# RWKV stage of a hybrid decoder step: the projection matmuls that are woven between its products, as 24 blocks of twelve per head pair instead of 48 blocks of six

## The reference, cut to what matters

```python
def step(S, inp):
    r_t, w_t, k_t, v_t, av_t, bv_t = inp
    sa = jnp.einsum('bhvk,bhk->bhv', S, av_t)
    S = S * w_t[:, :, None, :] + sa[..., None] * bv_t[:, :, None, :] + v_t[..., None] * k_t[:, :, None, :]
    return S, jnp.einsum('bhvk,bhk->bhv', S, r_t)
...
br = jnp.einsum('btnw,nwd->btnd', branches, p['w_branch'])
gates = jax.nn.sigmoid(gt.reshape(B, T, N_BRANCH, D_MODEL))
mix = jnp.sum(gates * br, axis=2) @ p['w_out']
```

## Time and profile before

| | |
|---|---|
| median of the three runs | 2814.52 us |
| span of the profiled execution | 2809.2 us |
| TensorE busy | 2484.5 us, 88% of the span |
| VectorE busy | 1546.0 us, 55% |
| ScalarE busy | 859.9 us, 31% |
| mean granted TensorE clock | 0.944 |
| start of s0t in pairs 1 and 6 (counted from 0) | 819.30 us, 1273.54 us |

### The profile page before, as it was taken

How to read it: one execution, slowest core, us unless ns; L and a number is a source line. 1 busy time by engine, 2 the same in 40 slices (tenths; PEclk the granted TensorE clock), 3 DMA queues, 4 the chain that set the end, 5 groups by cost and what they waited for, 6 DMA issues and landing times.

```text
span 2809.2 us, 50485 instructions
## 1 busy us (share of the span) xinstructions
PE 2484.5 (88%) x19707; PEld 2325.8 (83%) x19707; DVE 1546.0 (55%) x2210; ACT 859.9 (31%) x940; POOL 98.5 (4%) x171
## 2 busy tenths in 40 slices
PE   5999999456788998889989989599999999999976
PEld 4799999334677887777879989499999999999975
DVE  4533344513565566656663443766666666666665
ACT  4333333222222122222232333233333333333323
POOL 2000000010000000000000000000000000000001
PEclk9999999669899999999999999699999999999987
DMA  5544444244121223223235444144444444444441
GB/s 184 182 145 149 141 149 149 64 158 149 43 85 58 89 86 119 68 69 101 72 98 164 149 131 150 34 147 145 143 151 148 149 149 149 146 151 145 142 133 49
DMA packets 280233, 346.61 MB, mean 123 GB/s; under 512 B 6735, under 2 KB 240511, under 8 KB 278381
## 3 DMA queue, kind: packets, MB, share of 16 engines
q1 hardware_dynamic: 270365, 308.44, 34.5%
q0 software_dynamic: 9712, 36.30, 4.0%
q10 hardware_dynamic: 32, 0.01, 0.0%
HBM read 333.83 MB, written 10.89 MB: 123 GB/s over the span
## 4 chain that ended last, share of the span: by engine, by line
PE 71%; DVE 14%; issue 6%; ACT 5%; DMA 3%; DVEq 1%; POOL 1%; ACTq 0%; SPq 0%; POOLq 0%
PE bank L225 21%; PE bank L227 20%; PE bank L226 20%; PE bank L1015 5%; ACT hi L209 2%; DVE lo L216 2%; DMA work<-in_cache_mem_k 2%; DVE rw L1799 1%; DVE work L775 1%; PE bank L1384 1%; DVE q L701 1%; PE bank L424 1%; DVE rw L1797 1%; ACT rw L1741 1%; DMA raw<-in_w_in 0%
## 5 line engine op out<-in xcount | busy, mean ns | idle before, releaser
L225 PE MATMUL bank<-ah,hi 128*128 128x320 f32 x3232 | 1027.9, 318 | 45.2 <-DVE lo L216 21.1
L216 DVE TENSOR_TENSOR lo<-raw,hi 128x2048 fp32r<-128x2048 f32 x286 | 655.6, 2292 | 667.6 <-ACT hi L209 653.3
L226 PE MATMUL bank<-al,hi 128*128 128x320 f32 x3232 | 1006.5, 311 | 0.0
L227 PE MATMUL bank<-ah,lo 128*128 128x320 f32 x3232 | 1006.2, 311 | 0.0
L209 ACT ACTIVATE hi<-raw 128x2048 fp32r<-128x2048 f32 x286 | 547.6, 1915 | 1300.2 <-PE bank L227 1267.9
L225 PEld LDWEIGHTS bank<-ah,hi 128*128 128x128 f32 x3232 | 613.8, 190 | 65.9 <-issue 49.8
L226 PEld LDWEIGHTS bank<-al,hi 128*128 128x128 f32 x3232 | 614.5, 190 | 1.4 <-issue 0.2
L227 PEld LDWEIGHTS bank<-ah,lo 128*128 128x128 f32 x3232 | 614.0, 190 | 0.0
L225 PE MATMUL bank<-bh,hi 128*128 128x320 f32 x1088 | 346.9, 319 | 19.3 <-DVE bl L1814 18.5
L226 PE MATMUL bank<-bl,hi 128*128 128x320 f32 x1088 | 337.2, 310 | 0.0
L227 PE MATMUL bank<-bh,lo 128*128 128x320 f32 x1088 | 337.2, 310 | 0.0
(11 more groups left out here) (335 smaller groups left out, 1791.3 us busy)
## 6 DMA issues: line engine op xcount, KB each, us to landing
raw<-in_w_in SPq DMA_DIRECT2D x98, 1024.0 KB, 5.3
raw<-in_w_up SPq DMA_DIRECT2D x88, 1024.0 KB, 5.1
raw<-in_w_down SPq DMA_DIRECT2D x44, 1024.0 KB, 5.1
raw<-in_w_branch SPq DMA_DIRECT2D x24, 1024.0 KB, 5.5
raw<-in_w_out SPq DMA_DIRECT2D x16, 1024.0 KB, 5.4
raw<-in_w_mem_k SPq DMA_DIRECT2D x8, 1024.0 KB, 5.5
raw<-in_w_mem_v SPq DMA_DIRECT2D x8, 1024.0 KB, 5.1
work<-in_cache_mem_k POOLq DMA_DIRECT2D x8, 1024.0 KB, 5.3
```

The lines of the kernel that those rows point to most:

```text
L216: dve.tensor_tensor(lo[c % NS][:, :], raw[c % 2][:, :], hi[c % NS][:, :], ALU.subtract)\
L225: pe.matmul(out, a_hi, b_hi, start=first, stop=False)
L226: pe.matmul(out, a_hi, b_lo, start=False, stop=False)
L227: return pe.matmul(out, a_lo, b_hi, start=False, stop=last)
```

## The change

`pe_group_steps` hands back control after every fourth k instead of every second, so a block has twelve matmuls (4 k by 3 passes) instead of six, and there are 24 blocks per pair instead of 48. The table `STEPS` is written anew for them. No matmul, copy, transfer or buffer is added or taken away.

```diff
-                        if k % 2:
+                        if k % 4 == 3:
                             yield
...
-        STEPS = {PR["s0t"]: 1, PR["bonus"]: 2, PR["A"]: 1, PR["B"]: 7, PR["Bk"]: 1, PR["Cb"]: 1, PR["beT"]: 1,
-                 PR["kaT"]: 1, PR["R1"]: 1, PR["RT1"]: 1, PR["A4"]: 1, PR["B4"]: 3, PR["Q"]: 1, PR["Q2"]: 1,
-                 PR["QT2"]: 2, PR["QT4"]: 3, PR["W1"]: 2, PR["W2"]: 1, PR["S0"]: 1, PR["X1"]: 1, PR["X2"]: 1,
-                 PR["SA2"]: 2, PR["SA3"]: 1, PR["S3"]: 1, PR["S4"]: 2, PR["mean"]: 2, PR["tr1"]: 2, PR["var"]: 2,
-                 PR["g"]: 2}
-        assert sum(STEPS.values()) == 48
-        UNIT_END = [next(p for p in range(NPR) if sum(STEPS.get(x, 0) for x in range(p + 1)) >= 8 * (j + 1)) for j in range(6)]
+        STEPS = {PR["s0t"]: 1, PR["bonus"]: 1, PR["A"]: 1, PR["B"]: 2, PR["Cb"]: 1, PR["beT"]: 1, PR["A2"]: 1, PR["R1"]: 1,
+                 PR["A4"]: 1, PR["R2"]: 1, PR["Q"]: 1, PR["Q2"]: 1, PR["QT4"]: 1, PR["W1"]: 1, PR["W2"]: 1, PR["S0"]: 1,
+                 PR["X1"]: 1, PR["SA2"]: 1, PR["S3"]: 1, PR["S4"]: 1, PR["mean"]: 1, PR["tr1"]: 1, PR["g"]: 1}
+        assert sum(STEPS.values()) == 24
+        UNIT_END = [next(p for p in range(NPR) if sum(STEPS.get(x, 0) for x in range(p + 1)) >= 4 * (j + 1)) for j in range(6)]
```

## The result

The changed kernel takes 2884.33 us (median of 4 runs, 2876.15 to 2886.96), the kernel before 2812.87 us beside it. The ratio is 1.0242, with a 95% interval of 1.0226 to 1.0258: slower by 68 us by the ratio, by 71.5 us between the medians.

What follows compares the result with a forecast made beforehand. TensorE was taken to set the pace, through its matmuls, changes between matmul kinds and waits for VectorE. Waits and places (+34 us) and the clock (+21 us) added 55 to 2814.5, giving 2870 us, range 2845 to 2890.

Steps and rivals of the forecast that it cites:

- Units served elsewhere (part 2): In each pair, units' hi and lo served at other products: 11.9 us of new waits, 5.9 us gone.
- five of six places of service: Opening claim on the pair: the change moves five of six places where serving a unit costs TensorE its full length.
- The wait ahead of the next pair's first block: Ahead of s0t at the turn of a pair: the wait of 1.35 us for lo goes.
- the 1.4 for X2, SA3 and Bk: These copies lose the block ahead of them while VectorE has other work: 1.4 us of new wait per pair together.
- Fewer places (part 1): Six fewer places per pair where a block stands beside a product: 1.8 us given back, bounds nothing and 1.9.
- The 0.32 us per place: At Bk: a product beside a block costs 0.93 us, one without 0.61, so a place is worth 0.32.
- The sum of parts 1 and 2: Waits and places together: 11.9 - 5.9 - 1.8 = +4.2 us per pair, +34 us for eight pairs.
- The clock (part 3): After the wait at Q2: one more fall to 1.2 GHz in every pair, 2.6 us each, 21 us in all.
- the first rival: No further fall of the clock, perhaps as falls beside SA1 go with its wait: 2849 us, chance 0.22.
- The rival without a further fall: The same as the first rival: no further fall of the clock, only part 2 left, 2849 us, chance 0.22.
- The rival with two further falls: Waits at X0 and SA4, beside thin products, bring a second fall in each pair: 2890 us, chance 0.15.
- The faster rival: Service doesn't hold copies up at Q2, X0, RT1 and SA4 (9.3 us per pair): 2774 us, chance 0.03.

Runs made afterwards that it cites:

- two_places: tuned_a with its two groups of six blocks at s0t and A given in halves to s0t, bonus, A and B; 2724.31 us against 2725.29.
- fill_q2: The changed kernel with 27 more matmuls of 128x128 by 320, whose result nobody reads, ahead of TensorE's wait at Q2; 2861.03 us, ratio 1.0170.
- serve_u2: The changed kernel with only unit 2 served at QT2 instead of Q; 2841.16 us, ratio 1.0100.
- tuned_a: Against the kernel before: blocks of six placed by TensorE's waits, units served at QT, QT4, SA3, SA4, S4 and g; 2725.29 us, ratio 0.9675.

## Why the prediction was right, and where its sizes were off

The forecast of 2870 us had the direction and the mechanism; 2884 us was measured. The number is nearer than its terms were: two terms of the pair's sum were off in opposite directions, and a third fell short.

- **Units served elsewhere (part 2).** The opening says that the change moves five of six places of service; it moves four (units 1 to 4), and the sum rightly works with four. Forecast and measured waits in us: Q2 4.2 and 4.28, X0 2.3 and 2.19, SA4 2.1 and 2.00, SA1 0.4 and 0.43, RT1 1.1 and 0.91. The working from durations of the kernel before held within 0.2 us each. Smaller terms didn't. The wait ahead of the next pair's first block was to go; it shows 0.5 to 2.0 us in most pairs, ended by "issue", which the `lo` of the kernel before had covered. B waits nothing to 1.1 us instead of 1.2, and of the 1.4 for X2, SA3 and Bk only SA3's 0.97 came. Added up over pairs 1 to 6, TensorE's waits over 0.3 us are 9.0 us per pair before and 13.7 after: 4.7 more, where the terms gave 6.0 (11.9 less 5.9).
- **Fewer places (part 1)** gave back less than the 1.8 us per pair that were forecast. A pair is 8.4 us longer. Waits are 4.7 of it and the clock 3.9 (11.4 us more at the lower level, at 0.34), which leaves 0.2 us given back, an estimate with errors of several tenths. Six places at the 0.14 of two_places would give 0.8. The 0.32 us per place was read at one place and is too high for places beside s0t and A; between 64x64 products it was not tried by itself.
- **The sum of parts 1 and 2.** By the price, the 106 us more at the lower level cost 36 us. That leaves 71.7 - 36 = 36 us for waits and places; 34 were forecast. This agreement is partly luck, since the waits were put 1.3 us per pair too high and the places at least 1.0 us too high, and the two nearly cancel.
- **The clock (part 3) was mis-sized.** This is the term that made the forecast 14 us too low. It put one further fall of 6.8 us in each pair, 21 us in all; 36 us came. Six pairs at 0.92 have about 16 us at the lower level each (2 x 0.08 x 99.3) against 5 to 6 before, in two to four falls: after Q2, around X0, and between SA1 and S4. The kernel before has one fall in each of these pairs, beside SA0 or SA1. It went along with SA1's wait, as the first rival had considered, but the one at X0 took its place. The price per microsecond was nearly right (2.55 us for 6.5, 0.39, against 0.34), the number of falls wasn't. The rival with two further falls (2890 us) describes the run better, and it was given 0.15. The rival without a further fall (2849 us) is excluded by the clock after Q2 and by fill_q2. That waits of 2.0 to 2.2 us beside thin products would bring falls was named there and not taken.
- **The faster rival** (service doesn't hold copies up) is excluded by the waits themselves and by serve_u2.

## What to carry to other kernels

Where one table spreads filler work over a dependent chain and another engine's housekeeping hangs on the same table, moving the filler moves the housekeeping. Read which copy stands behind it before joining or moving blocks. In the changed kernel the `lo` that holds up Q2 is done at 1171.6 and first used at 1190.4, ahead of S0. A unit whose buffers aren't needed so soon should be served behind a copy that has cover, not as soon as it can be; in tuned_a two list entries are worth 68 us. A wait of TensorE can cost more than its length: those of 2.0 to 4.3 us here were followed by matmuls at the lower clock in most pairs, at 0.34 us for each microsecond.

## What was not expected of the hardware

The clock fell at short waits too: at X0's wait of 2.19 us in all eight pairs, and at SA4's of 2.00 us in four of seven. Small products stand around both. At the turn of pair 1 the changed kernel waits as long between blocks of 128x128 matmuls, and the clock stays at 1.00:

```profile
930.97 0.41 PE L225 MATMUL bank<-ah,hi 128*128 128x320 f32 x1 [1.98 <-issue]
...
930.97:937.97 7.00, 7.00 (x50) 6.39 (x52) 6.28 (x7) 1.25 (x1) 2.46 (x4) 1.00 0.19 57
```

So the length of a wait alone doesn't decide. That the products around it do is suggested by this and wasn't tried.

Work that nobody reads made the kernel faster: 41 matmuls per pair in two waits gave 37 us back.

The waits of 0.5 to 2.0 us ahead of a pair's first block, which the profile puts down to "issue", come at six of the seven turns from a pair to the next. The seventh, from pair 3 to pair 4, has none, nor in any of the eight other kernels where no `lo` covers it; there the program passes from one loop of four pairs into the next loop instead of turning back. At each of the six, a transfer of 16 KB on the queue that the profile calls "instruction" ends 1.6 to 2.0 us before TensorE goes on. So TensorE probably waits there for its own instructions. No run tried it.
